# Late projections behind the first tokens of a hybrid decoder step

## The reference, cut to what matters

```python
def gdn_branch(p, conv_buf, S0, lp, chunked):
    qkv = p[..., :GD_QKV]
    z = p[..., GD_QKV:GD_QKV + GD_WIDTH]
    ...
    qkv_c, new_buf = causal_conv(qkv, conv_buf, lp['gdn_conv_w'])   # four taps
    qkv_c = jax.nn.silu(qkv_c).astype(F32)
    q, k, v = (heads(t) for t in jnp.split(qkv_c, 3, axis=-1))
    q = l2norm(q, GD_EPS) * (GD_HEAD_DIM ** -0.5)
    k = l2norm(k, GD_EPS)
    ...                                                             # chunked delta rule: o, S
    on = on * jax.nn.silu(heads(z.astype(F32)))

def time_mix(h, ...):
    p = h @ lp['w_in']
    ya, shift_new, wkv = rwkv_branch(...); yb, conv_new, ssm = gdn_branch(...)
    merged = gates[..., :D_MODEL] * (ya @ w_branch_a) + gates[..., D_MODEL:] * (yb @ w_branch_b)
    return merged @ lp['w_out'], (shift_new, wkv, conv_new, ssm)

def peer_ffn(x, wq, subkeys, u_tab, v_tab):
    q = t @ wq                             # 8 heads, two halves of 128
    s1, i1 = lax.top_k(s[:, :, 0], 16); s2, i2 = lax.top_k(s[:, :, 1], 16)
    sc, ci = lax.top_k(cand, 16)           # 16 of the 256 pairs
    gate = jax.nn.softmax(sc, axis=-1)
    hpre = jnp.einsum('tkd,td->tk', u_tab[e_b], x_b)
    return jnp.einsum('tk,tkd->td', g_b * jax.nn.gelu(hpre), v_tab[e_b])

def decoder_layer(...):
    x1 = layer_norm(DN_ALPHA * x + mix, ln1_g, ln1_b)
    return layer_norm(DN_ALPHA * x1 + peer_ffn(x1, ...), ln2_g, ln2_b), st
```

## Time and profile before

| | us |
|---|---|
| median of the timed runs (three) | 2181.68 |
| lowest, highest | 2179.1, 2185.19 |
| the profiled execution | 2167.24 |
| its span, first to last instruction | 2165.4 |
| PE, DVE, ACT, POOL busy | 1631.8, 1334.5, 394.7, 1025.7 |
| mean granted PE clock | 0.801 |
| first gather | 507.49 |
| moved by DMA | 718.93 MB |

### The profile page before, as it was taken

One profiled execution on the slowest core, in us unless ns is written; L12 is line 12 of the kernel. 1 busy time (PEld: TensorE's weight loads), 2 busy tenths in 40 slices (PEclk: granted clock), 3 DMA queues, 4 the chain that ended last, 5 costly groups with the idle time before them and its releaser, 6 DMA issues. The chain is left out here.

```text
span 2165.4 us, 32160 instructions
## 1 busy us (share of the span) xinstructions
PE 1631.8 (75%) x12789; PEld 979.4 (45%) x12789; DVE 1334.5 (62%) x2996; ACT 394.7 (18%) x751; POOL 1025.7 (47%) x1091
## 2 busy tenths in 40 slices
PE   7998989895978785798787758887775655656555
PEld 7886867763655552465454415655451000100000
DVE  4296187773645468856445678474557765676745
ACT  1322423232222011124101102230101000100000
POOL 0000020004745455475455556564556777777774
PEclk9998999996989996699988859998896555555555
DMA  9215276646999999899999998999999999999997
GB/s 263 68 49 152 71 216 214 224 146 208 378 386 399 399 400 411 306 370 399 399 400 402 403 405 322 390 400 399 401 401 403 399 404 407 400 404 395 406 407 276
DMA packets 271256, 718.93 MB, mean 332 GB/s; under 512 B 29219, under 2 KB 77822, under 8 KB 270074
## 3 DMA queue, kind: packets, MB, share of 16 engines
q0 software_dynamic: 151904, 554.59, 66.2%
q1 hardware_dynamic: 116552, 161.44, 21.7%
q10 hardware_dynamic: 2650, 0.85, 0.2%
HBM read 695.58 MB, written 21.30 MB: 331 GB/s over the span
## 5 line engine op out<-in xcount | busy, mean ns | idle before, releaser
L2517 DVE CUSTOM_DVE_ANT_0 arena<-arena,ps 128x1024 f32<-128x1024 f32 x520 | 634.5, 1220 | 526.5 <-DMA arena<-peer_u_dram,arena 268.0
L2450 POOL DMA_INDIRECT arena<-peer_u_dram,arena x520 | 504.6, 970 | 488.2 <-DVE arena L2517 398.1
L2455 POOL DMA_INDIRECT arena<-peer_v_dram,arena x520 | 493.9, 950 | 162.0 <-issue 148.7
L2570 PE MATMUL ps<-arena 48*128 48x512 bf16 x1040 | 259.1, 491 | 353.7 <-DVE arena L2517 338.3
L1317 PE MATMUL ps<-arena 128*128 128x128 f32 (+1 forms) x3072 | 432.3, 297 | 59.8 <-DMA arena<-w_in_dram 26.0
L1317 PEld LDWEIGHTS ps<-arena 128*128 128x128 f32 x3072 | 393.5, 205 | 170.0 <-issue 139.1
L2583 PE MATMUL ps<-arena 128*32 128x512 f32 x2080 | 392.9, 839 | 38.9 <-DMA arena<-peer_v_dram,arena 38.7
L2570 PEld LDWEIGHTS ps<-arena 48*128 48x128 bf16 x1040 | 53.5, 97 | 640.1 <-DVE arena L2517 559.1
L2551 ACT ACTIVATE arena<-arena 128x4 f32<-128x4 f32 x130 | 26.7, 205 | 897.1 <-DVE arena L2517 896.7
L387 PE MATMUL ps<-arena 128*128 128x260 f32 (+1 forms) x704 | 130.7, 348 | 4.1 <-ACT arena L465 4.1
L387 PEld LDWEIGHTS ps<-arena 128*128 128x128 f32 x704 | 115.6, 192 | 18.2 <-ACT arena L465 4.2
(11 more groups left out here) (368 smaller groups left out, 1795.3 us busy)
## 6 DMA issues: line engine op xcount, KB each, us to landing
arena<-w_in_dram SPq DMA_DIRECT2D x40, 1024.0 KB, 13.0
arena<-peer_wq_dram SPq DMA_DIRECT2D x32, 1024.0 KB, 13.6
arena<-w_out_dram SPq DMA_DIRECT2D x16, 1024.0 KB, 12.8
arena<-w_in_dram SPq DMA_DIRECT2D x30, 512.0 KB, 4.0
arena<-peer_u_dram,arena POOLq DMA_INDIRECT x520
arena<-peer_v_dram,arena POOLq DMA_INDIRECT x520
arena<-w_branch_a_dram SPq DMA_DIRECT2D x8, 1024.0 KB, 14.8
arena<-w_branch_b_dram SPq DMA_DIRECT2D x8, 1024.0 KB, 14.6
```

The costliest lines, as they stand in the source:

```text
L2450: pool.indirect_dma_start(e["U"][:, k % RU, :], None, a["peer_u"][0], offsets(k)).then_inc(u_in[k % RU // UB], 16)
L2455: pool.indirect_dma_start(e["V"][:, j % RV, :], None, a["peer_v"][0], offsets(j)).then_inc(v_in[j % RV // BATCH], 16)
L2517: dve.tensor_tensor_reduce(u, u, ps[:, 0:2, :], 1.0, 0.0, ALU.mult, ALU.add, e["hp"][:, c:c + 1]).then_inc(sem("e_h"), 1)
L2570: mm = pe.matmul(ps[:, h, :], e["pick"][r, i:i + 1].to_broadcast([3 * GROUP, P]), e["xp"][r, g % 2, :], start=True, stop=True)
```

## The change

Three things change. First, the late projections: the slabs of k and q come behind the front's in `SEQUENCE`, and their products fall into tile 0's choice. z, v, the sums, the units, the value convolution and the tails go from the opening into the token loop, as `late2_pe`, `late2_act`, `late2_dve` and `late2_sp`, with due times from z0 ahead of token 0 to the last tail before token 22. The convolution of k stays at the end of the opening; that of q goes ahead of the product of token 0. The slabs of z and v no longer pass through the ring; SP loads them at the end of the opening into room that is not used yet (four V rows and the buffer of saved operands), so V gathers 6 and 7 wait for z's spill and for v. The spills move from POOL's queue to SP's, and the three loads of tile 1's saved operands into the loop. Second, the first gathers: POOL issues the first six U gathers inside the opening, right behind `take_chosen`, which stands, with `turn_chosen`, behind q's second column tile. Third, the tables: tile 0's extra offsets are gone, tile 1's recurrence begins at token 22 instead of 3 and its first matmul waits for all of the late work and the tails' stores (`handed`); its front takes 45 tokens instead of 57, its choice 27 instead of 37. Tiles 2 and 3 begin 12 and 20 tokens later, with denser fronts, and tile 3's choice is denser.

```diff
-FIN = dict(A=0, R=4, B=8, K=12, V=16, gq=20, gk=24, gv=28, gg=32, bonus=36, z=40, x=44)
+FIN = dict(gv=0, z=4, A=8, R=12, B=16, K=20, V=24, gq=28, gk=32, gg=36, bonus=40, x=44)
...
-BEGINS = (-160.0, 3.0, 106.0, 224.0)
-STRETCH = (1.0, 1.0, 1.3, 1.3)
-CHOOSE_PACE = (0.55, 0.58, 0.78, 0.94, 1.2)
+BEGINS = (-160.0, 22.0, 118.0, 244.0)
+STRETCH = (1.0, 0.78, 1.0, 1.07)
+CHOOSE_PACE = (0.55, 0.42, 0.78, 0.78, 1.2)
...
-    return at + (0.0 if at < 50.5 else 9.0 if at < 54.4 else 18.0)
...
-SEQUENCE = [("f", i) for i in range(8)] + [("k", 0), ("k", 1), ("f", 8), ("f", 9), ("q", 0), ("q", 1)] + [("f", i) for i in range(10, 16)] + [
-    ("keys", 0)] + [("f", i) for i in range(16, NSLAB)] + [("v", 0), ("v", 1), ("z", 0), ("z", 1)]
+SEQUENCE = [("f", i) for i in range(16)] + [("keys", 0)] + [("f", i) for i in range(16, NSLAB)] + [("k", 0), ("k", 1), ("q", 0), ("q", 1)]
...
+Z_AT, V_AT, KN_AT, QN_AT, CONV_AT, TAILS_AT = (-1.5, -0.6, 1.7, 3.7), (5.7, 7.7, 9.7, 11.7), -0.38, -0.3, 13.7, 18.7
...
 def late_pe(m, pe):
...
+            late_piece(m, pe, g, ct, [ring[number % SLOTS] for number in numbers])
+            if (g, ct) == ("q", 1):
+                pe.wait_ge(m["sem"]("s_done"), 2)
+                pe.wait_ge(m["sem"]("sel_done"), 2)
+                turn_chosen(m, pe, front(m, 0))
...
+def late_slabs(m, sp):
+    sp.wait_ge(m["sem"]("s_wkv_out"), 32)
+    for g in "zv":
+        for h in range(2):
+            sp.dma_start(m["lb"][g + "slab"][h], late_source(m, g, h)).then_inc(m["sem"]("b_slab_" + g), 16)
...
+def late2_pe(m, pe):
...
+    yield from gate(0)
+    yield from gate(1)
+    yield from sums("k", KN_AT)
+    yield from sums("q", QN_AT)
+    yield from gate(2)
+    yield from gate(3)
+    for ct in range(4):
+        yield V_AT[ct]
+        if ct == 0:
+            pe.wait_ge(sem("b_slab_v"), 32)
+        late_piece(m, pe, "v", ct, lb["vslab"])
...
+def late2_dve(m, dve):
+    yield -1.5
+    for ct in range(4):
+        late_convolve(m, dve, "q", ct)
+    for g, at in (("k", 0.1), ("q", 1.1)):
...
             st.link(dve.reciprocal(sq[:, h], sq[:, h]))
...
+def handed(m, eng):
+    eng.wait_ge(sem("b_out"), taken(len(LATE_UNITS)))
+    eng.wait_ge(sem("b_unit"), 2)
...
+    eng.wait_ge(sem("tails_saved"), 64)
...
+            pool.wait_ge(sem("sel_taken"), 2)
+            pool.wait_ge(sem("x1_saved"), 16 * 13)
+            for k in range(RU):
+                gather_u(m, pool, k)
...
+            if j == 6:
+                pool.wait_ge(sem("b_spilled_z"), 16 * (NT - 2))
+            elif j == 7:
+                pool.wait_ge(sem("b_mm"), late_number("v", 3))
```

More of the change, by code:

```diff
@@ L1963, in taken @@
 def taken(u):
[L1965 to L1985 removed]
+    return u + sum(g in "zc" for g, _ in LATE_UNITS[:u])
@@ new lines, in late_bank, with late_free, late_piece @@
+def late_bank(g, ct):
+    u = late_number(g, ct)
+    return (2 if g in "kq" else FB) + (u - 1) % 2
+def late_free(m, pe, g, ct):
+    u = late_number(g, ct)
+    if u < 3:
+        pe.wait_ge(m["sem"]("rows_out"), len(ROUNDS) + 1)
+    else:
+        pe.wait_ge(m["sem"]("b_out"), taken(u - 2))
+def late_piece(m, pe, g, ct, slabs):
+    late_free(m, pe, g, ct)
+    for h in range(2):
+        for k in range(4):
+            mm = pe.matmul(m["ps"][:, late_bank(g, ct), 0:NL_], slabs[h][:, k, ct * P:(ct + 1) * P], m["xT"][:, 4 * h + k, P:NP],
+                           start=(h == 0 and k == 0), stop=(h == 1 and k == 3))
+    mm.then_inc(m["sem"]("b_mm"), 1)
@@ L2003, in sums @@
             if ct == 0:
-                pe.wait_ge(sem("b_sq"), 1 if g == "k" else 2)
-            free(g + "n", ct)
-            pe.matmul(ps[:, bank(g + "n", ct), 0:NL_], const(m, "ones"), lb["sq"][g][:, ct], start=True, stop=True).then_inc(done, 1)
-    yield from project_late("k")
-    yield from project_late("q")
-    yield from sums("k")
-    yield from sums("q")
-    yield from project_late("v")
-    for ct in range(4):
-        yield begins(0) + L_AT["conv"] + 1.2 * ct
-        pe.wait_ge(out, taken(late_number("v", ct)))
-        if ct == 0:
-            pe.wait_ge(sem("b_taps"), 16)
-        free("c", ct)
-        for tap in range(4):
-            mm = pe.matmul(ps[:, bank("c", ct), 0:NL_], lb["taps"][:, 4 * ct + tap], lb["raw"][1][:, ct, tap:tap + NL_], start=(tap == 0), stop=(tap == 3))
-        mm.then_inc(done, 1)
@@ L2022, in late_pe @@
-    yield from project_late("z")
-    for n, (j0, j1, _) in enumerate(TAILS):
-        yield begins(0) + L_AT["tails"] + 0.5 * n
-        if n == 0:
-            pe.wait_ge(out, taken(late_number("z", 3)))
-            pe.wait_ge(sem("b_tail"), 3)
-        else:
-            pe.wait_ge(sem("tail_out"), n)
-        for j in range(j0, j1):
-            mm = pe.transpose(ps[0:TAIL, 2 + (j - j0) // 4, (j - j0) % 4 * P:((j - j0) % 4 + 1) * P], m["tail"][:, j, :], const(m, "ident"))
-        mm.then_inc(sem("tail_mm"), 1)
@@ L2091, in late_act, with late_convolve @@
                            ).then_inc(sem("b_taps"), 1)
-    yield from take("v")
-    for ct in range(4):
-        yield begins(0) + L_AT["conv"] + 1.2 * ct + 1.1
+def late_convolve(m, dve, g, ct):
+    sem, raw, conv, st = m["sem"], m["lb"]["raw"][g], m["lb"]["conv"][g], m["front_steps"]
+    dve.wait_ge(sem("b_out"), taken(late_number(g, ct)))
+    dve.wait_ge(sem("b_halo"), 1 if g == "k" else 2)
+    w = lambda tap: param(m, "gdn_conv_w", tap * QT + LATE_ROW[g] + ct)
+    st.link(dve.tensor_scalar(conv[:, ct], raw[:, ct, 3:], w(3), None, ALU.mult))
+    for tap in (2, 1, 0):
+        st.link(dve.scalar_tensor_tensor(out=conv[:, ct], in0=raw[:, ct, tap:tap + NL_], scalar=w(tap), in1=conv[:, ct], op0=ALU.mult, op1=ALU.add))
+    dve.sem_inc(sem("b_conv"), 1)
@@ L2638, in _ @@
         def _(pe):
[L2639 removed]
+            in_turn(late2_pe(m, pe), experts_pe(m, pe), *(s(m, pe, n) for n in later for s in (recur_r_pe, recur_g_pe, front_pe)),
                     states_pe(m, pe), rows_pe(m, pe))
```

363 lines of the change are left out of this document (188 added, 175 removed).

## The result

| | before | after |
|---|---|---|
| median of the timed runs, us | 2179.09 | 2187.75 |
| lowest, highest (20 runs each) | 2168.74, 2185.19 | 2176.24, 2204.33 |
| ratio, 95% interval | | 1.0051 [1.0036, 1.0065] |
| span of the profiled execution | 2165.4 | 2186.6 |

The changed kernel is half a per cent slower. The forecast was 2173 us, faster; 2187.75 lies in the range, the sign is wrong. The median of before is now that of 20 runs. The profiled execution of before, 2167.24 us, is shorter than all of these 20, while that of after, 2188.45 us, lies at its median, so the two profiles are 21 us apart and the medians 8.7 us; where before spends the other 12 us in most executions no profile shows.

A forecast was written before the change was run, and what follows sets the result against it. Bound taken: full DMA engines while tokens run, underused in the opening. First 25 tokens 0, clock +5, rings -3, less starving -11 give -9 us: 2158 us profiled, scaled to 2173 us; range 2152 to 2202.

The forecast's parts named there:

- Opening: Ahead of the first gather: late work leaves the opening, 60.5 us less, first gather at 447 us.
- the front: Tile 0's front in the opening: k and q leave PE's queue; 33 us gained, floor 24, ceiling 43.
- The choice: Tile 0's choice in the opening: taps and evacuations move off ACT's way, 7.8 us gained.
- the turn: Transposes of tile 0's choice in the opening, moved behind q's second column tile: 15.3 us gained.
- First tokens: First 25 tokens: moved work spends the opening's gain again, 0 us (-7 to +11), token 25 at 580 us.
- After product 25: Token loop behind token 25: -11 us from less starving, and -3 us from rows already in hand.
- the place of recurrence 3: 1290-1350 us: recurrence 3 begins at token 246, after choice 2; gain 6 us (0 to 9).
- tile 1's denser front: Front 1 in 45 instead of 57 tokens, carried by three slots; with choice 3 costs 4 us (0 to 8).
- Choice 1's steeper pace: Choice 1 in 27 instead of 37 tokens: 8 us lost in its last 15 tokens, leaving a gain of 9.
- The third: Rival, 10%: front held at its 24 us floor, token 25 slips 9 us or more, +5 to +10: 2190 us.
- the first rival: Rival, 27%: nothing gained; choice 1's pace starves the loop 13 us or more, second piece at half clock: 2181 us.
- Cold PE: Rival, 18%: PE at the lower clock through all six late pieces in the first tokens, +31 instead of +5: 2199 us.

The follow-up runs named there:

- the tables of tiles 2 and 3 alone: The kernel before with only the new table entries of tiles 2 and 3: 2165.73 us, 0.9951 of before.
- the norm later too: The kernel before with the new tables of tiles 2 and 3 and the layer norms 16 tokens later: 2157.69 us, 0.9903 of before.
- the same kernel with the norm later: The changed kernel with the layer norms of tiles 0 and 1's outputs 16 tokens later: 1.0020 of before.
- half pieces: The changed kernel with the eight z and v pieces cut to 8 of their 16 matmuls: 1.0021 of before.
- front 0.86: The changed kernel with units spread behind products 2, 4, 6, 8, and tile 1's front stretched 0.86 (was 0.78), choice pace 0.36 (was 0.42): 1.0011 of before.

## Why the prediction was wrong

- **Opening: -60.5 foretold, -49.4 measured.** The term that was mis-sized is the front: 33 taken, 24.0 measured (the choice starts at 388.09 instead of 412.1), the floor that the text had named. Between 297 and 365 us PE waits for DVE and for slabs, by its waits in 296 to 366 us (total, times, longest):

```profile
PE ps L1314 <- DVE arena L1520: 6.8, 1, 6.8
PE ps L1314 <- DMA arena<-w_branch_a_dram: 6.1, 1, 6.1
PE ps L1314 <- DVE arena L1512: 6.0, 3, 2.3
PE ps L1314 <- DMA arena<-w_in_dram: 3.1, 1, 3.1
```

  DVE, with the sample's steps between the front's, takes 12.8 us of these (6.8 + 6.0), more than the one step of 9.20 that the text left in the way. The slabs, which the estimate left out, come too late by 9.2 (6.1 + 3.1). The choice gave 8.0 (7.8), the turn 13.8 (15.3), the gathers' place 3.6 (4.4).
- **First tokens: the mechanism and sizes held.** From the first gather, product 0 came after 28.7 us (28 foretold), product 2 after 57.9 (60), product 14 after 101.5 (103), product 25 after 137.4 (133). A pair took 7.4 us (7.1). Two pieces ran long at a lower clock, 7.95 and 7.14 instead of 5.43 us: 4.2 of the 5 us allowed. So product 25 is 13 us behind before instead of 5, 9 us of the opening's shortfall standing in it, and at 595.5 us it is past the 592 that the prediction had named as a sign of being wrong. The moved 5.4 MB held no product up that could be seen: from 447 to 580 us the engines moved 208 GB/s at a share of .59. A spill landed after 13.5 us (median) instead of 3.5. The full engines under which the rule of the Trainium skill (DMA: Bandwidth & Descriptors, Issuing engines are not separate DMA queues) would have had a price weren't there over that stretch.
- **After product 25: -14 foretold, +8 measured** (21.3 - 13.1), and here is the step that failed: the place of recurrence 3, which was to gain 6 us (11 of the hitch, less 5 for the start of the recurrence). The hitch went, but the tokens with the recurrence lose 18.2 us instead of 2.6, so that products 120 to 280 lose 8.3 us more than before (15.6 - 7.3). No step of the sum looked at what else ACT does in the tokens to which recurrence 3 was moved. Where the clock came back, with the tables of tiles 2 and 3 alone, the same stretch ran at 369 GB/s and lost 9.4 us; with the norm later too, at 376 GB/s, 7.3 us.
  The second term is tile 1's denser front. Three slots were to carry its slabs, for at most 4 us together with choice 3; its tokens lose 9.1 us more. Choice 1's steeper pace was sized well: 8 us were to stay lost at its end, 8.7 did. Together 10 us are lost (8.3 + 9.1 - 7.4; 8 by the products' times, as the rates are rounded and slightly fewer bytes move) where 11 were to be gained.
- **Rivals.** The third had the front at its floor of 24 us and product 25 late, as it came, and its 2190 us lies near 2187.75. That is in part luck, since it kept the 11 us gained behind product 25, and a slip of 9 us alone would make its sum 0 and not +5 to +10. In the first rival -9 + 5 + 5 is +1 and not -1, 2183 us instead of 2181. That 2187.75 lies in the range of 2152 to 2202 speaks for the width of the range and not for the sum.
- **Cold PE.** The rival had the mechanism and the wrong place. It is not the first tokens but the end of recurrence 3, worth 12.4 us between products 260 and 280 against the same kernel with the norm later (77.0 - 64.6), 6.7 us by the medians. The Trainium skill (TensorE: Matmul & The Clock Gate, HAM oscillation) says that bursts behind waits start cold; the row at 1420 us agrees.
- **Spread.** That executions would differ more was not foretold: the 20 runs lie within 28 us, those of before within 16. The nine runs from 2188.34 us up had a mean granted clock of .784 to .792, the eleven below it .793 to .796, so the longer ones had PE at the lower clock for longer; in which stretches, no profile shows.

## What to carry to other kernels

A transfer that starts earlier is worth only as much as its reader starts earlier: follow the first reader's own queue before a lead at the gathers is counted. When a step is moved to other tokens, list what every in-order engine does in those tokens; here a norm with a table load on ACT made PE wait 3.6 us, and products 260 to 280 took 12.4 us more than without it. A profile is one execution: hold its time against the median before two profiles are compared. A change that bundles tables for several stages is split stage by stage before it is judged: one part was worth 11 to 13 us, and with the norm later 21 us (0.9903), while the whole was a loss.

## What the runs showed of the hardware

After the wait of 3.6 us in recurrence 3 PE's granted clock fell from 1.00 to .50 in all nine profiles that have it. What came behind differed between kernels with the same matmuls there: in six the clock was back at 1.00 after some 7 us, in three (after, half pieces, front 0.86) it stayed at .50 for some 27 us while PE was busy without a pause once its wait was over. What decides between the two isn't known. Products 260 to 280 take 7 to 10 us longer in the lasting case than where the clock came back (77.0 to 77.3 against 67.3 to 69.9).
